# Neighbourhood and grouped attention: values stationary, turned probabilities streamed

## The reference

```python
def hybrid_layer(x, ...):
    qa, ka, va, za, qb, kb, vb, zb, ga, gb = split_cols(einsum(rms_norm(x), w_in))
    oa = gqa_attention(rope(norm(qa)), rope(norm(ka)), va) * silu(za)   # 8 heads, 2 key heads
    ob = neighbourhood_attention(qb, kb, vb, rpb) * silu(zb)            # 8 heads of 64
    ya, yb = oa @ w_o_attn, ob @ w_o_na
    return x + (sigmoid(ga) * ya + sigmoid(gb) * yb) @ w_out
# gqa_attention: softmax(q k^T / 8) v over all 272 tokens
# neighbourhood_attention: a query sees 4 rows x 16 columns of near keys, with a bias, and the 16 meta keys;
#   softmax over both together, then the weighted sum of the values
# meta queries have their own rows; layer 1 needs none of them
```

## Time and profile before

| | |
|---|---|
| median of 3 executions | 1154.15 us (1152.80 to 1155.03) |
| the profiled execution's own time | 1154.66 us |
| its span in the profile | 1152.8 us |
| mean granted clock of TensorE | 0.996 |
| attention stretch of layer 0, of layer 1 | 74 to 202 us, 303 to 419 us |
| TensorE, VectorE, ScalarE, GpSimd busy | 97%, 71%, 54%, 22% |
| HBM read | 182.5 MB, 159 GB/s over the span |
| chain of work that ended last | TensorE 82%, VectorE 13%, ScalarE 2% |

### The profile page before, as it was taken

How to read it: one execution, slowest core, us unless ns; L and a number is a source line. 1 busy time by engine, 2 the same in 40 slices (tenths; PEclk the granted TensorE clock), 3 DMA queues, 4 the chain that set the end, 5 groups by cost and what they waited for, 6 DMA issues and landing times.

```text
span 1152.8 us, 23113 instructions
## 1 busy us (share of the span) xinstructions
PE 1120.4 (97%) x9124; PEld 1098.1 (95%) x9124; DVE 823.8 (71%) x1842; ACT 619.3 (54%) x1154; POOL 254.9 (22%) x213
## 2 busy tenths in 40 slices
PE   6999999999999999999999999999999999999997
PEld 6999999999999999999999999988999999999997
DVE  6964356779544678787766799677856887777666
ACT  6555545564655547544444554464455564444555
POOL 1056553200665714000000007400770000000000
PEclk9999999999999999999999999999999999999999
DMA  6454332354533434555445654324543545554551
GB/s 244 157 183 147 111 119 93 135 183 138 186 133 119 153 119 169 211 199 202 161 176 182 214 184 147 110 74 167 186 162 139 196 166 189 190 179 157 195 209 37
DMA packets 38778, 185.04 MB, mean 161 GB/s; under 512 B 12552, under 2 KB 14984, under 8 KB 20240
## 3 DMA queue, kind: packets, MB, share of 16 engines
q1 hardware_dynamic: 38672, 183.57, 45.4%
HBM read 182.49 MB, written 1.06 MB: 159 GB/s over the span
## 4 chain that ended last, share of the span: by engine, by line
PE 82%; DVE 13%; ACT 2%; issue 2%; DMA 1%; POOL 0%; DVEq 0%; SPq 0%; ACTq 0%
PE line L2216 51%; PE result L2216 18%; DVE w_lo L1377 4%; PE line L2529 2%; PE turn L2373 1%; PE result L2407 1%; PE score L2350 1%; PE score L2548 1%; PE stat L2407 1%; PE score L2354 1%; PE score L2216 1%; DMA h<-in_tokens 1%; ACT w_hi L882 1%; DVE prod L1699 1%; PE line L2226 0%
## 5 line engine op out<-in xcount | busy, mean ns | idle before, releaser
L864 POOL TENSOR_TENSOR w_lo<-raw,w_hi 128x512 fp32r<-128x512 f32 x168 | 224.5, 1368 | 542.3 <-ACT w_hi L882 542.2
L1377 DVE TENSOR_TENSOR w_lo<-raw,w_hi 128x512 fp32r<-128x512 f32 (+2 forms) x546 | 338.4, 664 | 3.3 <-ACT w_hi L917 2.0
L2216 PE MATMUL line<-x_hi,w_hi 128*128 128x256 f32 (+1 forms) x1048 | 310.2, 296 | 15.9 <-DVE x_lo L1429 9.0
L2216 PE MATMUL line<-x_hi,w_lo 128*128 128x256 f32 (+1 forms) x1048 | 299.4, 286 | 0.0
L2216 PE MATMUL line<-x_lo,w_hi 128*128 128x256 f32 (+1 forms) x1048 | 299.0, 285 | 0.0
L882 ACT ACTIVATE w_hi<-raw 128x1024 fp32r<-128x1024 f32 (+2 forms) x178 | 179.7, 1009 | 91.8 <-PE line L2216 36.7
L2216 PEld LDWEIGHTS line<-x_hi,w_hi 128*128 128x128 f32 x1048 | 199.5, 190 | 23.2 <-issue 16.6
L2216 PEld LDWEIGHTS line<-x_lo,w_hi 128*128 128x128 f32 x1048 | 199.4, 190 | 1.4 <-issue 0.5
L2216 PEld LDWEIGHTS line<-x_hi,w_lo 128*128 128x128 f32 x1048 | 199.9, 191 | 0.0
L2216 PE MATMUL line<-y_hi,w_hi 128*128 128x256 f32 (+1 forms) x656 | 192.6, 294 | 1.0 <-DVE y_lo L1437 0.3
L2216 PE MATMUL line<-y_hi,w_lo 128*128 128x256 f32 (+1 forms) x656 | 185.4, 283 | 0.0
(11 more groups left out here) (393 smaller groups left out, 2294.0 us busy)
## 6 DMA issues: line engine op xcount, KB each, us to landing
raw<-in_weights SPq DMA_DIRECT2D x144, 1024.0 KB, 4.8
raw<-in_weights SPq DMA_DIRECT2D x32, 704.0 KB, 4.0
rel_raw<-in_rpb SPq DMA_DIRECT2D x64, 24.0 KB, 4.8
h<-in_tokens SPq DMA_DIRECT2D x2, 544.0 KB, 6.4
raw<-in_weights SPq DMA_DIRECT2D x2, 512.0 KB, 6.0
rbias<-bias_by_distance SPq DMA_DIRECT2D x8, 128.0 KB, 4.5
out<-wide SPq DMA_DIRECT2D x4, 256.0 KB, 2.9
consts<-in_consts SPq DMA_DIRECT2D x1, 960.0 KB, 7.1
```

The costliest lines, as they stand in the source:

```text
L864: pool.tensor_tensor(w_lo[:, u % CUT, at], raw[:, u % RAW, at], w_hi[:, u % CUT, at].bitcast(F32), ALU.subtract).then_inc(lo_pool, 1)
L1377: dve.tensor_tensor(w_lo[:, u % CUT, at], raw[:, u % RAW, at], w_hi[:, u % CUT, at].bitcast(F32), ALU.subtract).then_inc(lo_cut, 1)
L2216: ins = pe.matmul(bank[:, 0:n], stay, move[:, first + k, 0:n], start=(k, m) == (0, 0), stop=(k, m) == (depth - 1, 2))
```

## The change

- `values` of the A and B jobs: the values are now stationary (64 columns, or 128 for the shared tile) and the turned probabilities stream (128 columns). The result has features on its partitions and lies in `result_bank` 0 or 1, by pair of heads in turn, one half of the columns per tile.
- The exponential of these jobs is written back to the score bank in PSUM. A new VectorE step `evenly` for job t-1, ahead of `maxes` of job t, takes the reciprocal of the job's own sum and multiplies the powers from PSUM into `probs`. `turn` waits for it (`evened`) instead of for the exponential, and so does the next use of the score bank.
- The reciprocal and multiply behind the values, `head_out`, `pair_out` with its transpose and their semaphores go. `result_of` waits for the values themselves.
- TAIL is 2 instead of 3: results, rounding and remainders come one step earlier, and each layer has one step and one blank fewer (layer 0: 37 steps, blanks at 7, 11, 15, 19, 23; layer 1: 34, blanks at 7 and 11).
- Meta jobs keep their form; they lose their wait for the pairs, since `stat_bank` is no longer shared with them.

```diff
-TAIL = 3
+TAIL = 2
...
+        if len(_j) == 4:
+            SCORE_READ[(_l, *_j)] = ("evened", 2 * PAIRED[(_i, _j)] + _j[2] + 1)
...
-            _last[3] = ("normal", 2 * KT * (_i + 1))
+            _last[3] = ("pair_gated", KT * (_i + 1))
...
-    single_bank = [stat_bank, result_bank[1]]
-
-    pair_bank = result_bank[0]
+
+
+    def pair_bank(job):
+        return result_bank[(PAIRS * (job[0] == "B") + job[1]) % 2]
...
                 place = PLACE[(i, job)]
-                if place >= 2:
+                if place >= 2 and len(job) != 4:
                     act.wait_ge(turn_done, TURN_OF_JOB[LAST_OF_PLACE[place - 2]] + 1)
...
                 if len(job) == 4 and half == 0 and PAIRED[(i, job)] >= 2:
-                    act.wait_ge(normal, PAIRED[(i, job)] - 1)
+                    act.wait_ge(evened, 2 * (PAIRED[(i, job)] - 1))
                 first, keys = half * (P + HD), KEYS_B
                 if job[0] != "B":
                     first, keys = half * SECOND, TOK
-                act.activation(probs[0:m, place % 2, first:first + keys], score_bank[s % 2][0:m, 0:keys],
+                powers = score_bank[s % 2] if len(job) == 4 else probs[:, place % 2, first:]
+                act.activation(powers[0:m, 0:keys], score_bank[s % 2][0:m, 0:keys],
                                ACT.Exp, bias=top[0:m, n % 2, 0:1], scale=-1.0 if job[0] == "B" else 1.0,
                                accum_out=sum_at(job)[0:m, half:half + 1]).then_inc(exped, 1)
...
+            def evenly(job, n):
+
+                if len(job) != 4:
+                    return
+                dve.wait_ge(exped, n + 1)
+                pair, half, place = PAIRED[(i, job)], job[2], PLACE[(i, job)]
+                if place >= 2:
+                    dve.wait_ge(turn_done, TURN_OF_JOB[LAST_OF_PLACE[place - 2]] + 1)
+                first, keys = (half * (P + HD), KEYS_B) if job[0] == "B" else (half * SECOND, TOK)
+                own, powers = probs[:, place % 2, first:first + keys], score_bank[SCORE[(name, *job)] % 2][:, 0:keys]
+                link(dve.reciprocal(share[:, pair % 2, half:half + 1], total[:, pair % 2, half:half + 1]))
+                dve.tensor_scalar(own, powers, share[:, pair % 2, half:half + 1], None, ALU.mult).then_inc(evened, 1)
...
-                if len(job) != 4 or job[2] == 0:
-                    return
-                pair = PAIRED[(i, job)]
-                if pair >= 2:
-                    dve.wait_ge(paired, pair - 1)
-                dve.wait_ge(valued, n + 1)
-                link(dve.reciprocal(share[:, pair % 2, 0:2], total[:, pair % 2, 0:2]))
-                dve.tensor_tensor(head_out[:, pair % 2].rearrange("p (h d) -> p h d", d=HD),
-                                  single_bank[pair % 2][:, 0:P].rearrange("p (h d) -> p h d", d=HD),
-                                  share[:, pair % 2, 0:2].unsqueeze(2).to_broadcast([P, 2, HD]),
-                                  ALU.mult).then_inc(normal, 1)
...
-            def result_of(job):
+            def result_of(job, n):
 
                 if len(job) == 4 and job[2:] == (1, TILES - 1):
                     kind, c = job[:2]
                     part = 0 if kind == "A" else PAIRS
-                    dve.wait_ge(paired, PAIRED[(i, job)] + 1)
+                    dve.wait_ge(valued, n + 1)
                     dst, by = wide[:, part + c, 0:SEQ], silu[kind.lower()][:, c, 0:SEQ]
                     if kind == "A":
-                        dve.tensor_tensor(dst, pair_bank[:, 0:SEQ], by, ALU.mult).then_inc(pair_gated, 1)
+                        dve.tensor_tensor(dst, pair_bank(job)[:, 0:SEQ], by, ALU.mult).then_inc(pair_gated, 1)
                         return
-                    bank = pair_bank[:, 0:SEQ].rearrange("p (t r q) -> p t r q", t=TILES, q=Q_COLS)[:, :, ::-1, ::-1]
+                    bank = pair_bank(job)[:, 0:SEQ].rearrange("p (t r q) -> p t r q", t=TILES, q=Q_COLS)[:, :, ::-1, ::-1]
                     dve.tensor_tensor(by_columns(dst), bank, by_columns(by), ALU.mult).then_inc(pair_gated, 1)
...
             J, jobs = len(JOBS[i]), JOBS[i]
             for t in range(J + TAIL + 2):
+                if 1 <= t <= J:
+                    evenly(jobs[t - 1], JOB[i] + t - 1)
                 if t < J:
                     maxes(jobs[t], JOB[i] + t)
...
             def turn(job, n):
                 if len(job) == 4:
-                    pe.wait_ge(exped, n + 1)
+                    pe.wait_ge(evened, 2 * PAIRED[(i, job)] + job[2] + 1)
                 else:
                     pe.wait_ge(probs_ready, metas_to(i, n - JOB[i]))
...
                     kind, c, half, t = job
-                    pair = PAIRED[(i, job)]
-                    if half == 0:
-                        if pair >= 2:
-                            pe.wait_ge(normal, pair - 1)
-                        if metas_to(i, n - JOB[i]):
-                            pe.wait_ge(gated, (1, 1, 1, 2)[metas_to(i, n - JOB[i])])
+                    at = PAIRS * (kind == "B") + c
+                    if (half, t) == (0, 0) and at >= 2:
+                        pe.wait_ge(pair_gated, KT * i + at - 1)
                     v = va if kind == "A" else vb[:, :, c * P:(c + 1) * P]
-                    own = slice(half * HD, (half + 1) * HD)
+                    own = half_rows(half)
 
                     both = 0 if half else None
                     for b, (_, kt) in sorted(enumerate(tiles_of(job)), key=lambda b_t: b_t[0] == both):
-                        cols = slice(0, P) if b == both else own
-                        ins = pe.matmul(single_bank[pair % 2][:, cols], tn[:, b * P:(b + 1) * P], v[:, kt, cols],
-                                        start=(half, b) == (0, 0), stop=b == both)
+                        rows = slice(0, P) if b == both else own
+                        ins = pe.matmul(pair_bank(job)[rows, t * P:(t + 1) * P], v[:, kt, rows], tn[:, b * P:(b + 1) * P],
+                                        start=b == half, stop=b == both)
                 ins.then_inc(valued, 1)
-
-            def pair_out(job):
-
-                if (i, job) not in PAIRED or job[2] == 0:
-                    return
-                pair, (kind, c, _, t) = PAIRED[(i, job)], job
-                if t == 0 and (kind, c) != ("A", 0):
-                    pe.wait_ge(pair_gated, KT * i + PAIRS * (kind == "B") + c)
-                pe.wait_ge(normal, pair + 1)
-                pe.transpose(pair_bank[:, t * P:(t + 1) * P], head_out[:, pair % 2], ident).then_inc(paired, 1)
```

More of the change, by code:

```diff
@@ L441 @@
         if _k[0] == "layer1":
-            _last[4] = ("exped", JOB[1])
+            _last[4] = ("evened", 4 * KT)
         if _k[0] in ("layer1", "ffn0"):
@@ L480 @@
 METAS = sum(len(_j) != 4 for _i in range(DEPTH) for _j in JOBS[_i])
-def pairs_to(i, n):
-    return sum(JOB[k] + JOBS[k].index(j) <= JOB[i] + n for k, j in PAIRED if j[2] == 1)
 def metas_to(i, n):
@@ L596, in hybrid_blocks_kernel @@
     turn_done, turned_most = sem("turn_done"), sem("turned_most")
-    normal, paired = sem("normal"), sem("paired")
+    evened = sem("evened")
     valued, even_scores = sem("valued"), sem("even_scores")
@@ L640, in hybrid_blocks_kernel @@
                    y_used=y_used, h_ready=h_ready, act_raw=act_raw, act_up=act_up, down_used=down_used, exped=exped,
-                   maxed=maxed, normal=normal, rot_used=rot_used, pair_gated=pair_gated, gated=gated, low_ready=low_ready,
+                   maxed=maxed, evened=evened, rot_used=rot_used, pair_gated=pair_gated, gated=gated, low_ready=low_ready,
                    ckv_raw=ckv_raw, row_ready=row_ready, index_w_ready=index_w_ready, alpha_used=alpha_used,
@@ L661, in hybrid_blocks_kernel @@
     kb = a1.sb("kb", [PAIRS, TILES, 2, KEYS_B])
-    head_out = a1.sb("head_out", [2, P])
     va = a1.sb("va", [3, P])
@@ L1692, in layer @@
                 if TAIL <= t < J + TAIL:
-                    result_of(jobs[t - TAIL])
+                    result_of(jobs[t - TAIL], JOB[i] + t - TAIL)
                 if t >= TAIL + 2:
@@ L2380, in values @@
                 if job[0] == "Bm":
-                    pe.wait_ge(normal, pairs_to(i, n - JOB[i]))
+                    pe.wait_ge(gated, 2 * i + 1)
                     for hd in range(HEADS):
@@ L2442, in layer @@
                     values(jobs[t - 2], JOB[i] + t - 2)
-                if t >= TAIL:
-                    pair_out(jobs[t - TAIL])
             two_lines([(name, "yb", 0), (name, "yb", 1)], W, y_of[name], PAIRS, PAIRS, (0, PAIRS),
```

1 line of the change is left out of this document (removed).

## The result

| | before | after |
|---|---|---|
| median of 4 executions each | 1154.01 us (1152.80 to 1155.03) | 1170.88 us (1169.99 to 1171.73) |
| span of the profiled execution | 1152.8 us | 1169.9 us |
| mean granted clock of TensorE | 0.996 | 0.996 |

The ratio is 1.0143, with a 95% interval from 1.0128 to 1.0157. The change costs 16.9 us; the forecast was a gain of about 1. The time lies far outside the stated range of 1150.0 to 1156.8. Between profiled executions the part behind the attention differs by some 5 us (739.7 to 745.3 over all kernels), with TensorE's granted clock at 0.5 for 0 to 10 us between 650 and 790 us, so differences of 1 to 3 us between kernels are better read from the attention stretch, which ran at 1.00, than from the medians.

The account below looks back on a forecast made before the run. TensorE, busy 97% of the span, was taken as the bound. Gains of 3.7 us less losses of 2.9 gave 0.8 us below the profiled 1154.66: 1153.9, about 1153.3 against the median; 8-in-10 range 1150.0 to 1156.8.

Parts of the forecast that it names:

- I take 0.11, no change: Value matmuls turned round: 192 passes streaming 128 columns over 64 were priced at 0.11 us each, as before.
- (C): Rival set up for the experiments, not in the prediction: streaming 128 columns instead of 64 per value pass costs the time.
- the second rival: Value passes paced by something other than 0.11 us; at 0.06, 1143.5 us, chance 0.05; partly (0.10), about 1151.3, chance 0.07.
- 0.07 us each: Price of each of the 32 removed transposes back; 21 of them counted, 1.5 us gained.
- price of 0.34 and 0.44 us: Length taken for VectorE's new tensor_scalar from PSUM in front of the turn, at 176 and 272 columns.
- The second steps: Second step of each layer: the scale, behind a silu, ends after TensorE is ready; loss 0.6 us, twice, 1.2 us.
- The first blanks: Blank at t = 7 of each layer: scale behind the silu makes the turn late; 0.4 us, twice, 0.8 us lost.
- The later blanks: Blanks after the first: the turn already waits for ScalarE's copy and the scale is done before; loss nothing.
- the third rival: VectorE bounds the turn at blanks and short lines; a scale of 0.9 to 1.4 us costs 6.7 us, 1160; chance 0.14.
- the 2.9 of the sum: Total predicted losses, in us, where TensorE meets the scale: second steps, first blanks and short lines.
- The hole at 168 us: Layer 0, exponential late behind the window bias, a hole of 0.84 us; TAIL 2 was to gain 0.6 us.
- The layer ends' wait for the gate: First yb line waits 0.76 us for the last ya line's gate multiply; last values inside it gain 0.9 us in all.

Follow-up runs that it names:

- padded: The changed kernel with each half's values stored once more beside zeros, making every value matmul of the A and B jobs 128 wide: 1157.65 us, ratio to before 1.0031.
- product64: The kernel before plus one fp32 matmul per pair of heads, 64 columns of `head_out` stationary and the identity streaming, ahead of the transpose: 1166.20 us.
- extra128: The kernel before plus one more transpose per pair of heads, of all 128 columns of `head_out`: 1157.27 us, ratio 1.0027.
- extra64: The kernel before plus one more transpose per pair of heads, of only the first 64 columns of `head_out`: 1156.84 us, ratio 1.0021.
- padded_tail3: The padded kernel with TAIL back at 3, all else the same: 1160.01 us, ratio to before 1.0049.

## Why the prediction was wrong

1. **The step that failed is the value matmuls: "I take 0.11, no change".** The spacing was right: narrow passes follow each other after 0.109 us. What the sum lacked is the way between the forms, and that term measures 19.4 us (after against padded), 0.33 in each of the 58 jobs whose values stand between a full turn and a score. It shows in the starts of the passes on PE: 0.20 us instead of 0.11 into the other width, twice per job; 0.16 instead of 0.11 to the first narrow operand's second pass; and 0.10 more to the second pass of the first wide matmul behind. That is the score (0.25 or 0.33 instead of 0.15 or 0.23) or, in a second half, the value matmul of the shared tile (0.21 instead of 0.11). The padded form in turn is 1.6 us slower between value passes than the kernel before (C): with 64 columns streaming, the second pass of a job's first value matmul had followed after 0.06 us, that of the shared tile after 0.165 and the others after 0.11; with 128 all take 0.11. I had read the pace before from loads, which run ahead, and not from matmuls.
2. The trace of before had this wait. The only 64 by 64 passes, which I used for the lower bound, stand between wide ones, and I took their spacing among themselves and not what stood around them. PEld just past the rows in the kernel before:

```profile
105.90 0.42 PEld L2391 LDWEIGHTS stat<-turned,va 128*64 128x64 f32 x6 [0.17 <-issue]
```

The 0.17 at the end of this row, met once or twice per job, was the loss.
3. **The Trainium skill** states the rule in TensorEngine Tiling (Array Packing), Key Properties: a change of the tiling mode, not of the tile alone, empties the engine, and different tiles load and multiply in parallel. The runs agree with both: 0.24 us (product64) and 0.33 (the jobs of the change) for one way in and out, and eight passes in the time of four. What they show is the wait; what the array does in it is in no trace. Its list of Restrictions says that column tiling excludes the transposing mode for fp32 input; that fits the narrow transpose that didn't wait, and the trace can't tell whether it is the reason. The Trainium skill's rule on load time by columns (TensorE: Matmul & The Clock Gate, LDWEIGHTS), weighed in the prediction as the second rival, spoke for the change; the spacing of 0.109 us refutes that use of it.
4. **Transposes.** 0.07 us each was low: a transpose moves the next pass by 0.11 us, and 32 more of them cost 3.2 us (extra128; 2.8 in extra64), 0.10 each, and in "values, transpose, score" padded has 4.0 us less than before.
5. **The scale.** Its length came out a little above the price of 0.34 and 0.44 us, 0.40 and 0.50, with the narrow spread I relied on (count, ns min/median/max):

```profile
L1609 DVE TENSOR_SCALAR probs<-score,share x64: 399/450/504, 79.0 to 432.6; 128x272 f32<-128x272 f32 x32, 128x176 f32<-128x176 f32 x32
```

The second steps lost 0.57 and 0.50 us, forecast 0.6. The first blanks lost far more than the 0.4 forecast, 0.86 in layer 1 and 1.52 in layer 0:

```profile
106.05 1.51 DVE L1655 SCALAR_TENSOR_TENSOR silu_b<-th,silu_b 128x272 f32<-128x272 f32 x1
107.49 0.15 DVE L1608 RECIPROCAL share<-total 128x1 f32<-128x1 f32 x1
107.67 0.50 DVE L1609 TENSOR_SCALAR probs<-score,share 128x272 f32<-128x272 f32 x1
...
108.23 0.20 PEld L2375 LDWEIGHTS turn<-consts,probs 128*128 128x128 f32 x2 [1.52 <-DVE probs L1609]
108.59 0.42 PEld L2392 LDWEIGHTS stat<-turned,va 128*64 128x64 f32 x6 [0.17 <-issue]
```

The silu in front, with two operands in SBUF, stood 1.51 us beside a GpSimd subtraction that had begun 0.06 us earlier; it took 0.55 before, beside one that was 1.02 us old and near its end. In both traces it takes 0.41 to 0.43 us where none runs. So part of this loss is how the two happened to meet. I had asked only whether the new instruction can be held off, not what stands before it. The later blanks, forecast to lose nothing, lost nothing: in the kernel as changed their waits fell from 0.57 to 0.30. Still the waits on the scale sum to 4.6 us, under the 5 that I named, but only because the waits for the array gave VectorE time: in padded those put down to it are 6.9. In the padded form the scale costs 6.4 us: VectorE became the bound of the turn, as in the third rival, covered in the kernel as changed. That this is near the rival's price of 6.7 is luck, since its condition, a scale of 0.9 to 1.4 us, didn't come true. Against the 2.9 of the sum it is 3.5 more, which alone would have put the time at 1156.8, the very end of the range.
6. **TAIL.** The hole at 168 us closed as expected, though the next turn waits 0.30 for the scale. The layer ends' wait for the gate (1.5 us) is gone; in padded 0.7 of it stand. The gains are in the traces and small; as a time only 1.2 us of the 2.2 forecast are shown (padded_tail3, stretch).
7. The sum in the stretch: 19.4 + 1.6 lost in the array, 4.0 won with the transposes, 0.1 before the turns: 16.9, where 17.1 was measured.

## What to carry to other kernels

Before you turn operands round, look whether the new stationary operand has a different width class from its neighbours on TensorE: here (fp32, 128 rows) a narrow true matmul between wide ones cost its stream and 0.24 to 0.33 us more, however busy the engine looked. Where narrow ones can't be avoided, put those of different output partitions together, where they ran side by side, or pad them with zeros. Both took back most of the loss here, and neither beat the kernel before. When a large cost sits on one engine, it can cover lateness on the others: with 19.4 us removed here, 5.2 of lateness showed.

## What the runs showed of the hardware that was not expected

- A true fp32 matmul with 64 stationary columns among 128-wide ones: 0.20 us instead of 0.11 from the pass before, and as much on the way back; a transpose of 64 columns: 0.11, no wait.
- Two series of 64-wide matmuls to different output partitions ran side by side without being interleaved in the program: 8 passes in 0.42 us.
- PE's busy time showed nothing of it (126.2 of 128 us busy, with 73 matmuls fewer in the window).
